# Last two output tiles before a layer norm by 256-token parts, feed-forward width in groups of 8, 6 and 8 chunks

## The chip, the cores and the metric

One core of a Trainium2 chip runs the whole program. The metric is the device time of one execution in microseconds. In the program and the rows PE is the tensor engine, PEld its weight load, DVE VectorE, ACT ScalarE, POOL GpSimd and SP the engine that issues most transfers.

## What is computed

Two blocks in a row on 512 tokens of width 1,024. The first has depth 2; each layer is feed-forward, mixer (state space, forgetting attention, short convolution), feed-forward, each followed by a layer norm of the residual sum:

```python
def layer_norm(x, g, b):
    xf = x.astype(jnp.float32)
    mu = jnp.mean(xf, axis=-1, keepdims=True)
    var = jnp.mean(jnp.square(xf - mu), axis=-1, keepdims=True)
    return ((xf - mu) * lax.rsqrt(var + LN_EPS) * g + b).astype(x.dtype)
...
def modulate(x, shift, scale):
    return x * (1.0 + scale) + shift
...
def swiglu_ffn(h, w_in, w_out):
    gate, up = jnp.split(h @ w_in, 2, axis=-1)
    return (jax.nn.silu(gate) * up) @ w_out
...
        h = modulate(x, mod[:, 0, 0], mod[:, 0, 1])
        y = swiglu_ffn(h, ffn1_w_in[l], ffn1_w_out[l])
        x = layer_norm(ALPHA * x + 0.5 * mod[:, 0, 2] * y, ln_g[l, 0], ln_b[l, 0])
```

The feed-forward is 2,816 wide, 22 chunks of 128. The second block has two layers, grouped-query attention and latent attention, each with a squared-relu feed-forward of width 4,096; its first layer also carries a context stream of 256 tokens. `mod` comes from a product of a vector with large modulation weights (`ada`).

## The kernel before

**Layout.** Activations lie transposed, 128 rows of the width by all tokens; a chunk is 128 rows, and there are 8. Each product is made of three passes over a split of both operands into a rounded part and its remainder (`passes`, L1934 to L1936), so weights and activations exist as `w_hi`, `w_lo`, `h_hi`, `h_lo`, `hid_hi`, `hid_lo`. A linear is a row of units of weights, each with `tpu` output tiles that are sums over `kc` chunks. For each unit a transfer brings `raw`, ScalarE rounds it (`w_hi`, L1262), VectorE subtracts (`w_lo`, L2750); there are two slots for weights, so unit i is rounded when unit i-2 has been used. The tiles leave PSUM by VectorE: L2817 or L3142 adds a tile times its gate to `x_lat`.

**Feed-forward.** The width is cut in groups (`FF_GROUPS`, 12 and 10 chunks). For each group a `gateup` linear makes the hidden chunks (ScalarE gate, VectorE product, ScalarE rounding, VectorE remainder `hid_lo` L2804), then an output linear of 8 tiles, one unit each, adds to `x_lat`. The last group's output linear ends in the norm. VectorE makes the partial sums of the modulation (`ada_acc`, L2833 and L2836) after each unit of the early linears; its last two units of a linear come in `finish`, behind the first units of the next linear. The tensor engine sums them (L1928) after the first and the second unit of the next linear.

**The norm.** Parts are 256 tokens: two of `lat`, and one of `ctx` where both streams run. Towards the end of the output linear GpSimd adds the first four tiles (`x_sum`), the tensor engine multiplies them by `ones` (`first_mean`, L1942), ScalarE copies that first mean, and VectorE subtracts it from x (`shifted`, L3015), so that squares can be made early: ScalarE squares, GpSimd adds squares (`ssum`). The last tile is computed by parts. `totals_begun` (L1950 to L1958) multiplies `x_sum`, `ssum` and the squares of tile 6 with `ones`; `close` (L1966, L1969) adds the last tile and its squares. VectorE then has mean and variance (`deviation`, L3053 to L3058), ScalarE the root, VectorE the reciprocal (L3065), then centred and scaled groups of chunks (L3076, L3087), ScalarE `h_hi`, GpSimd the same in full (L1056), VectorE `h_lo` (L3095). The next linear begins with part 0 on the first chunks of `h_lo` (`after_norm`); inside its chunk 3 the totals of part 1 are closed.

**The context step** (`ctx_in`, VectorE's `context_in`) prepares the context's first input between the two linears of the last feed-forward group of the first block. It waits for all modulation sums counted up to its place. Before a linear that feeds a norm, VectorE waits for `x` of all parts (`x_ready`); before another linear right behind the context step the wait leaves out the context's part (`parts_behind`).

Each engine runs its own program in written order; semaphores join them.

## Time and profile before

| | us |
|---|---|
| median of three runs | 3,999.8 |
| lowest and highest run | 3,988.89 and 3,999.96 |
| span of the profiled execution, first to last instruction | 3,992.6 |
| tensor engine busy in it | 3,831.8 |
| mean granted clock of the tensor engine | 0.978 |

The span is that of one execution; 7.2 us lie between it and the median of the runs. A busy tensor engine is one that has a multiplication in it. Idle time of an engine is printed in brackets before the instruction that ended it, with the instruction that released it.

### The profile page before, as it was taken

To read this page: it belongs to the slowest core of one execution; us is meant where nothing else is said; L and a number is where in the kernel's file an instruction comes from. 1 tells how busy PE (TensorE), PEld (TensorE's weight loads), DVE (VectorE), ACT (ScalarE), POOL (GpSimd) and SP (SyncE) were. 2 spreads that over 40 slices of the span, in tenths; PEclk is the share of its full clock that TensorE was granted. 3 is DMA by queue.
4 is the path that set the end of the run, shared out by engine and by line. 5 is a ranking of instruction groups with operands and counts; after the bars stand their busy time and mean duration, and the time that the engine had idled before them with its cause. 6 is when DMAs were issued, how large, how long until landed. Compare 5 with 4: busy or idle time off the path is not lost.

```text
span 3992.6 us, 51437 instructions
## 1 busy us (share of the span) xinstructions
PE 3831.8 (96%) x20234; PEld 3226.3 (81%) x20234; DVE 2539.0 (64%) x4095; ACT 1385.7 (35%) x1994; POOL 561.8 (14%) x559
## 2 busy tenths in 40 slices
PE   8999999999999999999998988989999999999998
PEld 6888877888888888788887678878888887888886
DVE  4666776754674677778445489686665367866335
ACT  2222334322232224432123179431221234853223
POOL 1000402300120012130004200150000141113001
PEclk8999999999999999999999999999999989999999
DMA  4554212344343432125322011213322112322221
GB/s 186 191 212 162 85 64 75 137 142 171 131 157 137 163 122 75 43 95 187 140 79 86 11 28 29 82 62 118 127 109 105 56 48 63 71 77 85 95 95 64
DMA packets 71229, 415.97 MB, mean 104 GB/s; under 512 B 8928, under 2 KB 12128, under 8 KB 30048
## 3 DMA queue, kind: packets, MB, share of 16 engines
q1 hardware_dynamic: 69744, 406.63, 29.3%
q10 hardware_dynamic: 1264, 6.29, 0.4%
q8 instruction: 151, 2.47, 0.3%
q14 instruction: 70, 0.57, 0.0%
HBM read 391.92 MB, written 2.10 MB: 99 GB/s over the span
## 4 chain that ended last, share of the span: by engine, by line
PE 81%; DVE 13%; ACT 2%; issue 2%; POOL 2%; DMA 0%; DVEq 0%; ACTq 0%; POOLq 0%
PE ps L1934 25%; PE ps L1936 24%; PE ps L1935 24%; DVE nmax L3716 2%; PE ps L1928 1%; DVE w_lo L2750 1%; PE ps L2644 1%; POOL sq_h_lat L1056 1%; DVE gp_lo L3733 1%; DVE rstd_lat L3065 1%; DVE x_lat L3076 1%; DVE x_lat L3087 1%; DVE mp_lo L3733 1%; DVE gprob L3728 1%; PE ps L2173 1%
## 5 line engine op out<-in xcount | busy, mean ns | idle before, releaser
L1934 PE MATMUL ps<-h_hi,w_lo 128*128 128x512 f32 (+2 forms) x2872 | 1096.6, 382 | 71.5 <-DVE h_lo L3095 49.6
L1936 PE MATMUL ps<-h_hi,w_hi 128*128 128x512 f32 (+2 forms) x2872 | 1073.0, 374 | 0.0
L1935 PE MATMUL ps<-h_lo,w_hi 128*128 128x512 f32 (+1 forms) x2800 | 1046.3, 374 | 0.0
L1262 ACT ACTIVATE w_hi<-raw 128x2048 fp32r<-128x2048 f32 (+3 forms) x262 | 457.8, 1748 | 1367.7 <-PE ps L1936 1329.7
L2750 DVE TENSOR_TENSOR w_lo<-raw,w_hi 128x2048 fp32r<-128x2048 f32 (+3 forms) x262 | 558.5, 2132 | 576.4 <-ACT w_hi L1262 576.1
L1934 PEld LDWEIGHTS ps<-h_hi,w_lo 128*128 128x128 f32 (+1 forms) x2872 | 548.9, 191 | 181.4 <-DVE h_lo L3095 46.0
L1936 PEld LDWEIGHTS ps<-h_hi,w_hi 128*128 128x128 f32 (+1 forms) x2872 | 548.3, 191 | 95.8
L1935 PEld LDWEIGHTS ps<-h_lo,w_hi 128*128 128x128 f32 x2800 | 535.5, 191 | 87.4 <-issue 0.5
L2836 DVE SCALAR_TENSOR_TENSOR ada_acc<-raw,c_act,ada_acc 128x256 f32<-128x256 f32 x1141 | 499.9, 482 | 16.8
L1934 PE MATMUL ps<-hid_hi,w_lo 128*128 128x512 f32 (+1 forms) x1272 | 498.9, 392 | 8.7 <-DVE w_lo L2750 6.8
L1936 PE MATMUL ps<-hid_hi,w_hi 128*128 128x512 f32 (+1 forms) x1272 | 490.2, 385 | 0.0
L1935 PE MATMUL ps<-hid_lo,w_hi 128*128 128x512 f32 (+1 forms) x1272 | 489.8, 385 | 0.0
L1934 PEld LDWEIGHTS ps<-hid_hi,w_lo 128*128 128x128 f32 x1272 | 240.1, 189 | 62.8 <-DVE w_lo L2750 8.9
L1936 PEld LDWEIGHTS ps<-hid_hi,w_hi 128*128 128x128 f32 x1272 | 239.7, 188 | 51.6
L1935 PEld LDWEIGHTS ps<-hid_lo,w_hi 128*128 128x128 f32 x1272 | 240.2, 189 | 50.4 <-issue 1.2
L1027 POOL TENSOR_TENSOR x_sum_lat<-x_lat 128x512 f32<-128x512 f32 x10 | 14.1, 1412 | 1867.2 <-DVE x_lat L3142 1319.4
L3142 DVE SCALAR_TENSOR_TENSOR x_lat<-ps,mod_lat,x_lat 128x512 f32<-128x512 f32 x70 | 52.4, 749 | 183.4 <-PE ps L1936 177.7
L1056 POOL TENSOR_SCALAR sq_h_lat<-x_lat,mod_lat 128x256 f32<-128x256 f32 x144 | 132.8, 931 | 173.5 <-DVE x_lat L3087 173.5
L3716 DVE TENSOR_REDUCE nmax<-ps 128x1 f32<-128x768 f32 x160 | 134.7, 842 | 8.2 <-PE ps L1936 5.7
L1304 ACT ACTIVATE hid_hi<-val_t 128x512 f32 (+1 forms) x88 | 55.6, 632 | 225.2 <-DVE val_t L2798 225.2
L1934 PE MATMUL ps<-hc_hi,w_lo 128*128 128x256 f32 x424 | 122.5, 289 | 8.2 <-DVE hc_lo L3095 8.2
L1440 ACT ACTIVATE h_hi<-x_lat,mod_lat 128x256 fp32r<-128x256 f32 x144 | 79.7, 594 | 128.8 <-DVE x_lat L3087 128.8
(486 smaller groups left out, 5969.8 us busy)
## 6 DMA issues: line engine op xcount, KB each, us to landing
raw<-ada SPq DMA_DIRECT2D x114, 1024.0 KB, 4.9
raw<-ffn_in SPq DMA_DIRECT2D x87, 1024.0 KB, 6.7
raw<-mlp_in SPq DMA_DIRECT2D x32, 1024.0 KB, 4.9
raw<-mlp_out SPq DMA_DIRECT2D x32, 1024.0 KB, 5.0
raw<-ffn_out SPq DMA_DIRECT2D x32, 768.0 KB, 5.4
raw<-ffn_out SPq DMA_DIRECT2D x32, 640.0 KB, 3.9
raw<-mix_p SPq DMA_DIRECT2D x14, 1024.0 KB, 4.8
raw<-mix_x SPq DMA_DIRECT2D x8, 1024.0 KB, 5.0
```

Of the source, the lines that this page charges most:

```text
L1056: eng.tensor_scalar(h32[:, k, part.cs], x[:, k, part.cs], g[:, k:k + 1], b[:, k:k + 1], ALU.mult, ALU.add).then_inc(s_n32, 1)
L1262: eng.activation(w_hi[:, slot, 0:ln.width], raw[:, slot, 0:ln.width], ACT.Copy).then_inc(s_whi, 1)
L1304: eng.activation(hid_hi[:, at(i), :], val_t[:, pos % 2, 0:SEQ].unsqueeze(1), ACT.Copy)\
L1440: eng.activation(hi[:, k, part.cs], x[:, k, part.cs], ACT.Identity, bias=b[:, k:k + 1], scale=g[:, k:k + 1]).then_inc(s_nhi, 1)
L1934: eng.matmul(out, lo_w, hi_x, start=first, stop=False, skip_group_check=True)
L1935: eng.matmul(out, hi_w, lo_x, start=False, stop=False, skip_group_check=True)
L1936: return eng.matmul(out, hi_w, hi_x, start=False, stop=last, skip_group_check=True)
L2750: eng.tensor_tensor(w_lo[:, slot, 0:ln.width], raw[:, slot, 0:ln.width], w_hi[:, slot, 0:ln.width].bitcast(F32), ALU.subtract).then_inc(s_ ...
L2836: ins = eng.scalar_tensor_tensor(acc, weights[:, :, k, :], c_act[:, c:c + 1], acc, ALU.mult, ALU.add)
L3142: a = eng.scalar_tensor_tensor(x, ps[:, tile_bank(ln, m, st), 0:NT[st]], MODT[st][:, ln.gate[st], 2 * DC + m:2 * DC + m + 1], x, ALU.mult, ...
L3716: eng.reduce_max(nmax[:, k % 8:k % 8 + 1], flat(2 * (k % 2))[:, 0:nk], AX_X, negate=True).then_inc(t_mx, 1)
L3733: eng.tensor_tensor(a.p[1][:, k % NPT, :], ps[:, B_PT + k % 2, :], a.p[0][:, k % NPT, :].bitcast(F32), ALU.subtract).then_inc(t_pl, 1)
```

## The change

- In every linear that feeds a norm, tiles 6 and 7 (before: only 7) are computed by parts: both tiles of part 0, then both of part 1, and of the context where there is one. Their evacuation, squares and closing sums become two per part (`last_tile`, `square_last`, `close_sum`, `close_squares`); tile 6 leaves `x_sum`, and `totals_begun` loses its third product. Part 0's totals are begun inside tile 6 of part 1. The tiles' sums are closed at chunk 3 of the next linear, the squares at chunk 4.
- `FF_GROUPS` is 8, 6, 8. Three pairs of linears in place of two; the last output linear has two tiles to a unit of 2,048 columns. No linear of the feed-forward is long enough for a loop any more.
- The first mean is taken in tile 4 ahead of its chunk 6 (before: behind tile 4); the shifts of pairs 0, 1 and 3 stand ahead of tile 4's evacuation.
- The modulation units keep their total; they fall on other linears. The context step comes behind the second group's `gateup`, whose six units all carry modulation units of two vectors, and ahead of an output linear that doesn't feed a norm.

```diff
 FF = 2816
-FF_GROUPS = (12, 10)
+FF_GROUPS = (8, 6, 8)
 FF2 = 4096
...
+def out_tiles(g):
+    return 2 if g + 1 == len(FF_GROUPS) else 1
 def schedule():
...
                 s.append(("ctx_in", Norm(None, None, 6, ("ctx",))))
-            lin(f"ffn{which}_out_{l}_{g}", DC, 1, nc, "resid", src="hid")
+            per = out_tiles(g)
+            lin(f"ffn{which}_out_{l}_{g}", DC // per, per, nc, "resid", src="hid")
...
-        def last_bank(ln, part):
-            if part.st == "ctx":
-                return 3
-            if len(ln.streams) == 1 and ln.norm.next and len(ln.norm.next.streams) > 1:
-                return 0 if part.c0 else 1
-            return 2 if part.c0 else tile_bank(ln, DC - 1, "lat") if len(ln.streams) > 1 else 3
+        def part_bank(ln, q, part):
+            nxt = ln.norm.next
+            if len(ln.streams) == 1 and nxt and len(nxt.streams) > 1:
+                return q if part.c0 else 2 + q
+            return tile_bank(ln, DC - 2 + q, part.st)
...
                            skip_group_check=True)
-                eng.wait_ge(s_sq, w.sq + 4 * ns)
+            def close_sum(norm, j):
+                part = norm.parts[j]
+                c = part.cs
+                eng.wait_ge(s_evac, part_evac(norm, j, 0))
+                eng.matmul(ps[:, B_SUM[j], 0:HALF], ones[:, :], X[part.st][:, DC - 2, c], start=False, stop=False,
+                           skip_group_check=True)
+                eng.wait_ge(s_evac, part_evac(norm, j, 1))
+                eng.matmul(ps[:, B_SUM[j], 0:HALF], ones[:, :], X[part.st][:, DC - 1, c], start=False, stop=True,
+                           skip_group_check=True).then_inc(s_total, 1)
+            def close_squares(norm, j):
+                part = norm.parts[j]
+                c = part.cs
+                eng.wait_ge(s_sq7, 2 * part.nidx + 1)
                 eng.matmul(ps[:, B_SQ, 0:HALF], ones[:, :], squares_of(norm, part.st)[:, DC - 2, c], start=False,
                            stop=False, skip_group_check=True)
-            def close(norm, j):
-                part = norm.parts[j]
-                c = part.cs
-                eng.wait_ge(s_evac, last_evac(norm, j))
-                eng.matmul(ps[:, B_SUM[j], 0:HALF], ones[:, :], X[part.st][:, DC - 1, c], start=False, stop=True,
-                           skip_group_check=True).then_inc(s_total, 1)
-                eng.wait_ge(s_sq7, part.nidx + 1)
+                eng.wait_ge(s_sq7, 2 * part.nidx + 2)
                 eng.matmul(ps[:, B_SQ, 0:HALF], ones[:, :], squares_of(norm, part.st)[:, DC - 1, c], start=False,
...
                             if p in norm.parts and k == 3 and closing:
-                                close(norm, closing.pop(0))
+                                close_sum(norm, closing[0])
+                            if p in norm.parts and k == 4 and closing:
+                                close_squares(norm, closing.pop(0))
                             if wide > 1 and n + 1 == len(parts):
...
                             eng.wait_ge(s_wlo2, ln.halved)
-                            eng.wait_ge(s_evac, last_evac(norm, 1))
+                            eng.wait_ge(s_evac, part_evac(norm, 1, 1))
                             for k in range(DC):
...
                                 slot = (ln.g0 + u) % 2
+                                if m == 4 and k == 6 and st == "lat":
+                                    first_mean(norm)
                                 mm = passes(ps[:, tile_bank(ln, m, st), 0:NT[st]], w_hi[:, slot, ws], w_lo[:, slot, ws],
...
                         mm.then_inc(s_tile, 1)
-                        if m == 4:
-                            first_mean(norm)
-                    u, q = divmod(DC - 1, ln.tpu)
-                    if q == 0:
-                        eng.wait_ge(s_wlo, ln.g0 + u + 1)
-                    eng.wait_ge(s_evac, ln.e0 + DC - ln.nbuf)
+                    eng.wait_ge(s_wlo, ln.g0 + ln.n)
                     for j, part in enumerate(norm.parts):
-                        if part.c0:
-                            eng.wait_ge(s_evac, tile_evac(norm, DC - 2))
-                        for k in range(ln.kc):
-                            if j == 1 and k == 2:
-                                close(norm, j - 1)
-                            mm = part_mm(u, q, part, k, last_bank(ln, part))
-                        mm.then_inc(s_tile if j + 1 == len(norm.parts) else s_last, 1)
-                        if j < 2:
-                            totals_begun(norm, j)
+                        for q in range(2):
+                            m = DC - 2 + q
+                            if j == 0:
+                                eng.wait_ge(s_evac, ln.e0 + m - ln.nbuf + 1)
+                            elif part_bank(ln, q, part) == part_bank(ln, q, norm.parts[j - 1]):
+                                eng.wait_ge(s_evac, part_evac(norm, j - 1, q))
+                            else:
+                                eng.wait_ge(s_evac, tile_evac(norm, DC - 3))
+                            for k in range(ln.kc):
+                                if j == 1 and q == 0 and k == 2:
+                                    totals_begun(norm, 0)
+                                    close_sum(norm, 0)
+                                if j == 1 and q == 0 and k == 4:
+                                    close_squares(norm, 0)
+                                mm = part_mm(ln.n - 1, q, part, k, part_bank(ln, q, part))
+                            mm.then_inc(s_tile if j + 1 == len(norm.parts) else s_last, 1)
+                        if j == 1:
+                            totals_begun(norm, 1)
                     if not norm.next:
-                        close(norm, len(norm.parts) - 1)
+                        close_sum(norm, 1)
+                        close_squares(norm, 1)
...
                     elif ln not in CUSTOM:
-                        linear(ln, sched[j - 1][1] if sched[j - 1][0] == "lin" else None, norm, before_it)
+                        prev = next(i for i in sched[j - 1::-1] if i[0] != "ctx_in")
+                        linear(ln, prev[1] if prev[0] == "lin" else None, norm, before_it)
                     if norm:
...
-            def shifted_sums(norm, k):
+            def shifted_sums(norm):
...
                 for i, st in enumerate(norm.streams):
-                    a = X[st][:, 4, :]
-                    if k == 5:
-                        eng.wait_ge(s_cent, w.cent + 2 * ns + 2 * i + 1)
-                    else:
-                        a = x_sum[st][:, :]
-                        eng.wait_ge(s_csum, w.csum + i + 1)
-                        eng.wait_ge(s_cent, w.cent + 4 * ns)
-                        eng.wait_ge(s_evac, tile_evac(norm, 6))
-                    eng.tensor_tensor(x_sum[st][:, :], a, X[st][:, k, :], ALU.add).then_inc(s_csum, 1)
-            def last_tile(ln, j):
-                part = ln.norm.parts[j]
-                x = X[part.st][:, DC - 1, part.cs]
-                if j == 0:
+                    eng.wait_ge(s_cent, w.cent + 3 * ns + i + 1)
+                    eng.tensor_tensor(x_sum[st][:, :], X[st][:, 4, :], X[st][:, 5, :], ALU.add).then_inc(s_csum, 1)
+            def last_tile(ln, j, q):
+                part, m = ln.norm.parts[j], DC - 2 + q
+                x = X[part.st][:, m, part.cs]
+                if j == 0 and q == 0:
                     eng.wait_ge(s_cent, w.cent + 4 * len(ln.norm.streams))
                 if j + 1 < len(ln.norm.parts):
-                    eng.wait_ge(s_last, w.last + j + 1)
+                    eng.wait_ge(s_last, w.last + 2 * j + q + 1)
                 else:
-                    eng.wait_ge(s_tile, ln.t0 + DC)
-                eng.scalar_tensor_tensor(x, ps[:, last_bank(ln, part), part.cs],
-                                         MODT[part.st][:, ln.gate[part.st], 3 * DC - 1:3 * DC], x, ALU.mult, ALU.add)\
+                    eng.wait_ge(s_tile, ln.t0 + m + 1)
+                eng.scalar_tensor_tensor(x, ps[:, part_bank(ln, q, part), part.cs],
+                                         MODT[part.st][:, ln.gate[part.st], 2 * DC + m:2 * DC + m + 1], x, ALU.mult, ALU.add)\
                    .then_inc(s_evac, 1)
...
                 parts = norm.parts
-                last_tile(ln, 0)
+                last_tile(ln, 0, 0)
                 if norm.next:
                     ahead(norm.next, 0, 1)
+                last_tile(ln, 0, 1)
                 deviation(norm, 0)
...
                             split_part(norm, part, g - 1)
-                        if g == 3 and j + 1 < len(parts):
-                            last_tile(ln, j + 1)
+                        if g == (1 if j == 0 and len(ln.streams) > 1 else 3) and j + 1 < len(parts):
+                            last_tile(ln, j + 1, 0)
+                            last_tile(ln, j + 1, 1)
                     if j + 1 < len(parts):
...
                         vectors_of(norm)
-                    elif m == 4:
-                        eng.wait_ge(s_evac, tile_evac(norm, 3))
-                        shifted(norm, (0, 1))
                     elif m == 5:
                         eng.wait_ge(s_evac, tile_evac(norm, 5))
-                        shifted(norm, (2, 3))
-                        shifted_sums(norm, 5)
-                    elif m == 6:
-                        shifted_sums(norm, 6)
+                        shifted(norm, (2,))
+                        shifted_sums(norm)
...
                     split_weights(ln, i, 0, i)
+                eng.wait_ge(s_evac, tile_evac(norm, 3))
+                shifted(norm, (0, 1, 3))
                 for m in range((ln.n - 2) * ln.tpu, (ln.n - 1) * ln.tpu):
                     tile(m)
-                for m in range((ln.n - 1) * ln.tpu, DC - 1):
-                    tile(m)
                 apply(ln, norm)
-                w.last += len(norm.parts) - 1
+                w.last += 2 * (len(norm.parts) - 1)
                 w.norm_done(norm)
```

The tensor engine at the first norm, from the end of part 0 of tile 7 (before), and there from inside part 1 of tile 6 (after; 6 products of it stand ahead of the first row). Names: `x_sum`, `ssum` are the sums made ahead, `x_lat,ones` a closing sum, `sq_h_lat,ones` one of squares. Before:

```order
L1950 MATMUL ps<-x_sum_lat,ones 128x256 [waits ln_shifted_summed]
L1955 MATMUL ps<-ssum_lat,ones 128x256 [waits ln_squares_summed]
L1958 MATMUL ps<-sq_h_lat,ones 128x256 [waits ln_squared]
L1934 MATMUL ps<-hid_hi,w_lo 128x256 [waits tile_evacuated]
L1935 MATMUL ps<-hid_lo,w_hi 128x256
L1936 MATMUL ps<-hid_hi,w_hi 128x256
L1934 MATMUL ps<-hid_hi,w_lo 128x256
L1935 MATMUL ps<-hid_lo,w_hi 128x256
L1936 MATMUL ps<-hid_hi,w_hi 128x256
L1966 MATMUL ps<-x_lat,ones 128x256 [waits tile_evacuated]
L1969 MATMUL ps<-sq_h_lat,ones 128x256 [waits ln_last_squared]
```

After:

```order
L1945 MATMUL ps<-x_sum_lat,ones 128x256 [waits ln_shifted_summed]
L1950 MATMUL ps<-ssum_lat,ones 128x256 [waits ln_squares_summed]
L1958 MATMUL ps<-x_lat,ones 128x256 [waits tile_evacuated]
L1961 MATMUL ps<-x_lat,ones 128x256 [waits tile_evacuated]
L1929 MATMUL ps<-hid_hi,w_lo 128x256
L1930 MATMUL ps<-hid_lo,w_hi 128x256
L1931 MATMUL ps<-hid_hi,w_hi 128x256
L1929 MATMUL ps<-hid_hi,w_lo 128x256
L1930 MATMUL ps<-hid_lo,w_hi 128x256
L1931 MATMUL ps<-hid_hi,w_hi 128x256
L1969 MATMUL ps<-sq_h_lat,ones 128x256 [waits ln_last_tiles_squared]
L1972 MATMUL ps<-sq_h_lat,ones 128x256 [waits ln_last_tiles_squared]
```

Line numbers of the same statement differ by a few. Behind part 0 came three opening products, six of part 1, and two closing ones; now two opening and two closing sums stand behind the first six, and two sums of squares behind the next six.

VectorE around the context step (`mod_ctx` to `hc_lo`). Before, from the last unit of the `gateup` linear:

```order
L2750 TENSOR_TENSOR w_lo<-raw,w_hi 128x1280 [waits weights_rounded]
L2798 TENSOR_TENSOR val_t<-ps,gate_t 128x512 [waits hidden_split,gate_activated]
L2804 TENSOR_TENSOR hid_lo<-val_t,hid_hi 128x512 [waits hidden_rounded]
L2992 TENSOR_TENSOR mod_ctx<-ps,par 128x24 [waits ada_unit_summed,ctx_loaded]
L2995 TENSOR_SCALAR mod_ctx<-mod_ctx 128x8 [waits modulation_steps]
L2997 TENSOR_SCALAR mod_ctx<-mod_ctx 128x8
L3095 TENSOR_TENSOR hc_lo<-sq_h_ctx,hc_hi 128x256 [waits h_modulated_of_part,h_rounded_of_part] x2
L3095 TENSOR_TENSOR hc_lo<-sq_h_ctx,hc_hi 128x512 [waits h_modulated_of_part,h_rounded_of_part] x3
L3142 SCALAR_TENSOR_TENSOR x_lat<-ps,mod_lat,x_lat 128x512 [waits tile_ready,x_ready_for_resid,tile_evacuated]
L2750 TENSOR_TENSOR w_lo<-raw,w_hi 128x1280 [waits weights_rounded]
```

After, from the second vector-pair modulation unit of `finish`:

```order
L2811 TENSOR_TENSOR val_t<-ps,gate_t 128x512 [waits hidden_split,gate_activated]
L2817 TENSOR_TENSOR hid_lo<-val_t,hid_hi 128x512 [waits hidden_rounded]
L2846 TENSOR_SCALAR ada_acc<-raw,c_act 128x256 [waits ada_unit_summed,weights_loaded_2]
L2846 TENSOR_SCALAR ada_acc<-raw,c_act 128x256
L2849 SCALAR_TENSOR_TENSOR ada_acc<-raw,c_act,ada_acc 128x256 [waits ada_partial_products] x14
L3005 TENSOR_TENSOR mod_ctx<-ps,par 128x24 [waits ada_unit_summed,ctx_loaded]
L3008 TENSOR_SCALAR mod_ctx<-mod_ctx 128x8 [waits modulation_steps]
L3010 TENSOR_SCALAR mod_ctx<-mod_ctx 128x8
L3101 TENSOR_TENSOR hc_lo<-sq_h_ctx,hc_hi 128x256 [waits h_modulated_of_part,h_rounded_of_part] x2
L3101 TENSOR_TENSOR hc_lo<-sq_h_ctx,hc_hi 128x512 [waits h_modulated_of_part,h_rounded_of_part] x3
L2763 TENSOR_TENSOR w_lo<-raw,w_hi 128x768 [waits weights_rounded,x_ready_for_resid,tile_evacuated]
L2830 SCALAR_TENSOR_TENSOR x_lat<-ps,mod_lat,x_lat 128x512 [waits tile_ready]
```

The step had nothing of the modulation ahead of it and a residual that waits for x behind it; now a modulation unit of two vectors stands right ahead, and behind it the split of a unit of 768 columns.

## Rows read from the trace of the kernel before

**Rows 1.** The page, part 1: busy us, share, instructions of each engine.

```profile
PE 3831.8 (96%) x20234; PEld 3226.3 (81%) x20234; DVE 2539.0 (64%) x4095; ACT 1385.7 (35%) x1994; POOL 561.8 (14%) x559
```

**Rows 2.** Waits of the tensor engine: total us, times, longest.

```profile
PE ps L1934 <- DVE h_lo L3095: 49.6, 42, 4.4
...
PE ps L1934 <- DVE w_lo L2750: 16.2, 7, 6.0
```

**Rows 3.** Timeline, tensor engine, first norm: start, us, operation, [idle before, releaser].

```profile
429.44 0.39 PE L1934 MATMUL ps<-hid_hi,w_lo 128*128 128x512 f32 x1
...
436.77 0.38 PE L1934 MATMUL ps<-hid_hi,w_lo 128*128 128x256 f32 x1 [0.20 <-DVE w_lo L2750]
...
440.42 0.59 PE L1950 MATMUL ps<-x_sum_lat,ones 128*128 128x256 f32 x2
...
440.85 0.59 PE L1955 MATMUL ps<-ssum_lat,ones 128*128 128x256 f32 x2
...
448.86 0.36 PE L1934 MATMUL ps<-h_hi,w_lo 128*128 128x256 f32 x1 [1.27 <-DVE h_lo L3095]
...
453.41 0.38 PE L1934 MATMUL ps<-h_hi,w_lo 128*128 128x256 f32 x1 [1.74 <-DVE h_lo L3095]
...
468.55 0.39 PE L1934 MATMUL ps<-h_hi,w_lo 128*128 128x256 f32 x1 [1.03 <-DVE h_lo L3095]
```

**Rows 4.** Timeline of VectorE in the same norm.

```profile
441.09 2.28 DVE L2750 TENSOR_TENSOR w_lo<-raw,w_hi 128x2048 fp32r<-128x2048 f32 x1
...
443.29 0.42 DVE L3053 TENSOR_SCALAR m_lat<-ps 128x256 f32<-128x256 f32 x1
...
444.20 0.42 DVE L3058 SCALAR_TENSOR_TENSOR rstd_lat<-ps,rstd_lat 128x256 f32<-128x256 f32 x1
...
456.66 0.42 DVE L3058 SCALAR_TENSOR_TENSOR rstd_lat<-ps,rstd_lat 128x256 f32<-128x256 f32 x1
```

**Rows 5.** Mixer norm: timeline; windows (PE, PEld, DVE, ACT, POOL busy; clock, DMA, GB/s).

```profile
705.67 0.60 PE L1950 MATMUL ps<-x_sum_lat,ones 128*128 128x256 f32 x2
...
722.40 0.42 DVE L3053 TENSOR_SCALAR m_lat<-ps 128x256 f32<-128x256 f32 x1 [1.32 <-PE ps L1966]
...
735.03 0.39 PE L1934 MATMUL ps<-h_hi,w_lo 128*128 128x256 f32 x1 [1.02 <-DVE h_lo L3095]
...
716.00:718.00 2.00, 1.59 (x6) 1.29 (x6) 1.36 (x3) 1.27 (x4) 2.00 (x3) 0.50 0.00 0
...
720.00:722.00 2.00, 2.00 (x10) 1.91 (x10) 1.07 (x2) 1.49 (x3) 1.43 (x2) 0.50 0.00 0
```

**Rows 6.** Timeline, end of a 12-chunk output linear: ScalarE, then VectorE.

```profile
917.91 1.92 ACT L1262 ACTIVATE w_hi<-raw 128x2048 fp32r<-128x2048 f32 x1 [6.88 <-PE ps L1936]
...
922.07 0.75 DVE L2817 SCALAR_TENSOR_TENSOR x_lat<-ps,mod_lat,x_lat 128x512 f32<-128x512 f32 x1
```

**Rows 7.** Timeline, start of a 10-chunk output linear: ScalarE, then VectorE.

```profile
1429.29 1.27 ACT L1262 ACTIVATE w_hi<-raw 128x1280 fp32r<-128x1280 f32 x1 [7.74 <-PE ps L1936]
...
1433.38 0.69 DVE L2804 TENSOR_TENSOR hid_lo<-val_t,hid_hi 128x512 fp32r<-128x512 f32 x1 [0.70 <-ACT hid_hi L1304]
...
1434.52 5.62 DVE L2836 SCALAR_TENSOR_TENSOR ada_acc<-raw,c_act,ada_acc 128x256 f32<-128x256 f32 x14
```

**Rows 8.** Timeline at the context step: three of VectorE, one of the tensor engine.

```profile
2091.70 0.18 DVE L2992 TENSOR_TENSOR mod_ctx<-ps,par 128x24 f32<-128x24 f32 x1
...
2098.05 0.93 DVE L3095 TENSOR_TENSOR hc_lo<-sq_h_ctx,hc_hi 128x512 fp32r<-128x512 f32 x1 [0.91 <-POOL sq_h_ctx L1056]
...
2104.70 0.75 DVE L3142 SCALAR_TENSOR_TENSOR x_lat<-ps,mod_lat,x_lat 128x512 f32<-128x512 f32 x1 [5.72 <-POOL x_ctx L1071]
...
2106.90 0.79 PE L1934 MATMUL ps<-hid_hi,w_lo 128*128 128x512 f32 x1 [5.96 <-DVE w_lo L2750]
```

**Rows 9.** Timeline, norm of both streams: tensor engine, then VectorE.

```profile
3203.11 0.59 PE L1950 MATMUL ps<-x_sum_lat,ones 128*128 128x256 f32 x2
...
3220.09 0.42 DVE L3058 SCALAR_TENSOR_TENSOR rstd_lat<-ps,rstd_lat 128x256 f32<-128x256 f32 x1
```

58 lines of the change are left out of this document (24 added, 34 removed).

## Prediction

> **What bounds the kernel now.** The page comes first: the tensor engine computes for 3,831.8 us of a 3,992.6 us span [rows 1], so only its idle time and the work put on it can move the time. The list of its waits says where the idle time lies: 49.6 us behind `h_lo` L3095, the last step of a layer norm, and 16.2 us behind `w_lo` L2750 [rows 2], of which one wait alone is 5.96 us, at the step that prepares the context [rows 8]. The feed-forward bodies between norms show no idle time worth a row. So the ten norms are what can be won, and the seams between linears, of which the change makes more, are what can be lost.
>
> A norm, read in the tensor engine's timeline [rows 3]: tile 6 of the output starts at 429.44; the first 256-token part of tile 7 runs from 436.77 to 440.42 (30 multiplications, 0.12 us each; a 512-token one starts every 0.23 us, 30 of them from 429.44); call its end T. Behind T come sums, the second part, sums again, and at 447.5 the engine is out of work. VectorE needs until 448.9 for the first `h_lo`, and the engine goes from wait to wait until 468.55. So from T+8.4 to T+28.1 the time is VectorE's chain, not the tensor engine's work. Two things move the end then: how early T comes, and how long the chain from T is.
>
> **The split of tiles 6 and 7.** T comes earlier, since half of tile 6 is put behind it. First norm: from the start of tile 6 to T there are 10.98 us [rows 3]. Groups of 8, 6, 8 make the last group 8 deep instead of 10, which moves 2 x 2 x 3 = 12 multiplications of 0.23 = 2.8 us elsewhere at no gain; afterwards two halves of 24 x 0.12 = 2.9, together 5.8. T is earlier by 10.98 - 2.8 - 5.8 = 2.4 us. With 8 chunks before and after: 8.4 before (24 x 0.23 + 24 x 0.12), so 2.6.
>
> The chain gets longer. (a) A multiplication with `ones` takes 0.43 us (one, in two instructions, from 440.42, the next from 440.85) [rows 3]. After T come now 6 products of tile 6 (0.7), `x_sum`, `ssum`, two closing sums (4 x 0.43 = 1.7), 6 products (0.7) and two sums of squares (0.9): 4.0 us, plus 0.3 to VectorE. Before, VectorE had the squares at 444.20, T+3.8 [rows 4]: +0.5. The 2.28 us `w_lo` that stood between last tile and mean [rows 4] now lies between the two last tiles and hides under the 2.9 us of products there, but the mean still waits for the sums, so nothing of it comes back. (b) VectorE adds a second last tile of part 1, 0.47: +0.5. (c) Part 1's sums are closed by the tensor engine inside the next linear, at its chunks 3 and 4. The third piece of `h_lo` lands at 453.4, T+13.0 [rows 3], now T+13.5; chunks 2 and 3 are 12 products (1.4), closing sum 0.9, then it waits for the fourth piece at T+16.4; chunk 4 is 0.7, the squares 0.9: T+18.0, with latency 18.2. VectorE would be there at 456.66 - 440.42 = 16.2 + 1.0 = T+17.2 [rows 4]. It waits 1.0. Sum: the chain is 2.0 us longer, last wait at T+30.1. The first norm gains 2.4 - 2.0 = 0.4 us.
>
> The mixer norm at 705.67 has 8 chunks before and after. It shows something else: at 716 and 720 the granted clock is 0.50, the lower level, 1.2 GHz, after the engine had sat idle in pieces from 712 on [rows 5]; its last wait ended at T+29.36 and VectorE waited 1.32 us for the engine's closing sum. With T 2.6 earlier and the last wait at T+30.1 at full clock, it gains 2.6 - 0.7 = 1.9. Four of the six norms that hand over to a 256-token part of one stream (the two mixers, the second feed-forward, the one after the second attention) show this drop; the two others don't. The stretch in which the engine mostly waits shrinks from six us (T+7 to T+13) to under four (T+9.9 to T+13.5), so I take the drop as gone except in one case in five. The Trainium skill (TensorE: Matmul & The Clock Gate, "HAM oscillation") prices a low stretch at half its length, here 3 us of at least 6; the rows say less, 29.36 against 28.13, 1.2 us, because the chain is VectorE's anyway. By the page the four norms would give 7 us more; the row decides.
>
> Sum for the ten norms: two first-type feed-forward norms 0.4 each; the second feed-forward norm, which had the drop, 1.8; mixers and latent attention 3 x 1.9; the one before the grouped attention 0 (a context part runs ahead of the closing, which puts VectorE 2.5 later and eats the 2.4); the last norm 1.3. That is 9.6. Less drops that stay or are new: -1.5.
>
> The two norms of **both streams** are different. T is earlier by 5.5 + 2.9 - 2.9 = 5.5 us, but the engine now has second part and context part behind it, 11.6 us with sums more, and comes to chunk 4 of the next linear, where part 1 is closed, at about T+22.5; before, VectorE had that at 3220.09 - 3203.11 = T+17.0 [rows 9]. 5.5 later: the gain is eaten by the place of the closing. Part 2 is closed the same way with two more products at 0.43 (0.86 at low clock) each for sum and squares: 1.5 to 2 later. I take -2 each, -4. Bounds: +3 (sums of squares ready in time and no drop) and -5.
>
> Norms together: 9.6 - 1.5 - 4 = **+4 us gained**.
>
> **The groups 8, 6, 8.** The products stay; 22 chunks are 22 chunks. What comes is one more seam in and out per feed-forward, four of each, and short linears.
>
> Out of a 6-chunk linear: its last tiles take 18 x 0.23 = 4.1. ScalarE rounds the next 2,048 columns from the end of tile 6 at 917.91 on, and VectorE has split them and evacuated tile 6 at 922.8, 4.9 later [rows 6]. An 8- or 12-chunk tile (5.5, 8.3) hides that; 4.1 doesn't. With 0.2 for the restart: 1.0 us, four times, **4.0**.
>
> Into a 6-chunk linear: the last hidden chunk was ready at 1434.07, 4.9 after the end at 1429.2 [rows 7]. With 768 columns rounding and splitting are 0.43 and 0.55 shorter: 3.9. The engine asks for chunk 6 after 15 x 0.23 = 3.4. 0.6 us each, in two plain seams **1.2**. In the third, whose modulation unit has two vectors, VectorE then spends 0.53 + 5.62 on it [rows 7] and is free at 10.1, while two tiles and a sum of 0.95 are through at 9.7; the engine waits 0.5 there and 0.7 more for tile 0's evacuation: **1.8**. The first feed-forward has a modulation unit with each tile of its 8-chunk linear, which gives VectorE nearly as much to do per tile as the tensor engine: **0.5** of lateness at the end, between 0 and 2.
>
> The fourth is the **context step**. Before: VectorE begins it at 2091.70, is through with `hc_lo` at 2098.98, then waits 5.72 for GpSimd's `x_ctx`, and the engine loses 5.96, with the restart 6.1 [rows 8]. Now the step stands before a linear that doesn't feed a norm, whose wait leaves the context part out, so the 5.72 is gone. But the six units ahead of it all carry modulation units of two vectors, and its first instruction waits for all of their sums; the last sum is made only after two tiles. Queue behind it on VectorE: the split of unit 2 and the evacuation of tile 0, for which the tensor engine waits. From the end of the last product: 0.6, VectorE free at 10.1, sum at 11.1, context step 7.3, split 0.95 and evacuation 0.7: 20.2. The engine was ready at 11.1: 9.1 lost, with 0.6 and 0.5 ahead of it 10.2. Net **4.1**.
>
> The **first mean** in the fifth tile, two chunks before its end, costs nothing: the sum of the first four tiles needs tile 3's evacuation and one addition of GpSimd, and the engine asks for it 18 x 0.23 = 4.1 us after tile 3. It keeps the shifts ahead of tile 4, where VectorE has slack. Loops that vanish cost or give nothing, since none shows in the rows.
>
> Costs: 4.0 + 1.2 + 1.8 + 0.5 + 4.1 = **11.6**. Net 7.6 slower: span 3,992.6 + 7.6 = 4,000.2. The median of three runs is 3,999.8, 7.2 over the span of the profiled execution; so 4,007.
>
> **Rivals.**
> Faster, *the chain isn't closed late*: if VectorE finds part 1's totals ready (engine at its chunk 4 earlier than I count), the eight one-stream norms give 2.6 - 1.0 each, 13, both-stream norms 3 each, 6, no clock drop 5: 24 - 11.6 = 12 faster, 3,988. For it: VectorE's chain was the bound everywhere. Against: at 722.40 it already waited 1.32 for that very sum [rows 5]. Chance 0.14.
> Slower, *closings at half clock*: one place, the closing of part 1 after T+13. If the engine falls to 1.2 GHz there, 12 + 6 products and four sums take double, VectorE gets the squares at T+21.4 instead of 18.2. 3.2 each; it decides from three norms on; in six of ten it is 17 to 19 in place of the 1.5: 4,023. For it: rows 5. Against: the shorter idle stretch. Chance 0.2.
> *The context step is cheap*: if its wait for the last sum fell under the two tiles, its 5.96 would go and nothing come: 10 better, 3,997, within the bound. Against: the order puts that sum behind tile 1. Chance 0.13.
> *The seams are free* (the 6-chunk tiles hide behind work I don't see): 5 better, 4,002. Chance 0.08.
> Forecast 0.45.
>
> **How the numbers follow.** About 0.3%, 12 us, is what a measurement here can tell from no change: 3,988 to 4,012. Faster than that: the first rival, 0.14. Slower: the second, 0.2, and the upper part of the forecast, 0.12, together 0.32. Same 0.54. The range takes in the bounds of both-stream norms (+10, -2), of the seams (-5) and three clock drops (+10): 3,989 to 4,023.
>
> **What would show it.** In the profile after: `h_lo` waits of the tensor engine fall in the one-stream norms (about 4 us each in place of 5), with the first wait (1.3) gone; VectorE waits for the closing squares of part 1; granted clock 1.00 through most norms; four waits on `w_lo` or `x_lat` of about 1 us where a 6-chunk linear ends; 9 us idle at the context step. It is wrong if the context step costs under 6 us, if the last wait of the first norm ends before T+29, or if the seams show no wait.

## The result and the profile after

| | before | after |
|---|---|---|
| median, us | 3,999.9 (4 runs) | 4,032.7 (4 runs) |
| lowest and highest run | 3,988.9 and 4,000.4 | 4,031.0 and 4,039.1 |
| profiled execution: span | 3,992.6 | 4,028.9 |
| tensor engine busy | 3,831.8 | 3,846.1 |
| mean granted clock | 0.978 | 0.979 |

The ratio is 1.0098 with an interval of 1.0086 to 1.011: 34 to 44 us slower. The forecast was 4,007 with a range up to 4,023, so the time lies outside it on the slow side. The spans differ by 36.3: 14.3 more busy and 22.0 more idle.

The page, part 1, of the changed kernel (to be read against [rows 1]):

```profile
PE 3846.1 (95%) x20494; PEld 3243.5 (81%) x20494; DVE 2532.9 (63%) x4141; ACT 1391.3 (35%) x2020; POOL 573.8 (14%) x559
```

Its waits of the tensor engine (total us, times, longest), against [rows 2]:

```profile
PE ps L1929 <- DVE h_lo L3101: 40.9, 38, 4.4
...
PE ps L1929 <- DVE x_lat L2830: 17.3, 9, 9.3
PE ps L1929 <- DVE w_lo L2763: 9.5, 2, 4.7
PE ps L1950 <- POOL ssum_lat L1047: 9.4, 7, 1.4
...
PE ps L1950 <- POOL ssum_ctx L1047: 6.1, 2, 3.1
...
PE ps L1929 <- DVE hid_lo L2817: 3.9, 4, 1.4
```

The waits for `h_lo` fell by 8.7 us and those for `w_lo` by 6.7. In their place stand 17.3 for evacuations (`x_lat`), 3.9 for hidden chunks, and 15.5 (9.4 and 6.1) for something that the list before did not have at all: GpSimd's sum of squares, `ssum`.

The first norm, tensor engine (start, us, operation, [idle before, releaser]); it answers to [rows 3]:

```profile
445.10 0.28 PE L1929 MATMUL ps<-hid_hi,w_lo 128*128 128x256 f32 x1
...
445.81 0.59 PE L1945 MATMUL ps<-x_sum_lat,ones 128*128 128x256 f32 x2
447.74 0.70 PE L1950 MATMUL ps<-ssum_lat,ones 128*128 128x256 f32 x2 [1.34 <-POOL ssum_lat L1047]
...
460.20 0.58 PE L1929 MATMUL ps<-h_hi,w_lo 128*128 128x256 f32 x1 [1.74 <-DVE h_lo L3101]
...
465.24 0.59 PE L1972 MATMUL ps<-sq_h_lat,ones 128*128 128x256 f32 x2
...
477.67 0.39 PE L1929 MATMUL ps<-h_hi,w_lo 128*128 128x256 f32 x1 [1.03 <-DVE h_lo L3101]
```

VectorE (first two rows) and GpSimd (last two rows) in the same norm, against [rows 4]:

```profile
439.60 0.75 DVE L3148 SCALAR_TENSOR_TENSOR x_lat<-ps,mod_lat,x_lat 128x512 f32<-128x512 f32 x1 [2.11 <-PE ps L1931]
...
450.99 0.42 DVE L3064 SCALAR_TENSOR_TENSOR rstd_lat<-ps,rstd_lat 128x256 f32<-128x256 f32 x1 [0.69 <-PE ps L1972]
...
438.12 2.67 POOL L1047 TENSOR_TENSOR ssum_lat<-ssum_lat,sq_h_lat 128x512 f32<-128x512 f32 x2
443.05 4.64 POOL L1047 TENSOR_TENSOR ssum_lat<-ssum_lat,sq_h_lat 128x512 f32<-128x512 f32 x2 [2.25 <-ACT sq_h_lat L1415]
```

The same in the kernel before, VectorE's evacuation of tile 5 and GpSimd's two additions:

```profile
429.64 0.75 DVE L3142 SCALAR_TENSOR_TENSOR x_lat<-ps,mod_lat,x_lat 128x512 f32<-128x512 f32 x1 [2.21 <-PE ps L1936]
...
433.64 4.23 POOL L1042 TENSOR_TENSOR ssum_lat<-ssum_lat,sq_h_lat 128x512 f32<-128x512 f32 x2 [2.25 <-ACT sq_h_lat L1410]
```

T, the end of part 0, is 445.10. Tile 5 starts to leave PSUM at 439.60. Its shift, squares and GpSimd's two additions (4.64) end at 447.69, 8.1 us later; the product that needs them is due 6.7 us after 439.60. Before, the additions ended 8.2 us after tile 5 as well (437.87), but the product came only 11.2 us after it (440.85), since a whole tile 6 lay between. The squares reach VectorE at T+5.9, the last wait ends at T+32.6.

Windows of 2 us, two in the same norm and one behind the context step (busy time of PE, PEld, DVE, ACT, POOL; clock; DMA share; GB/s):

```profile
461.00:463.00 2.00, 2.00 (x11) 2.00 (x11) 1.82 (x3) 1.02 (x3) 0.57 (x1) 0.50 0.00 0
463.00:465.00 2.00, 2.00 (x12) 1.83 (x12) 0.59 (x2) 2.00 (x3) 0.90 (x2) 0.86 0.02 4
...
2016.00:2018.00 2.00, 2.00 (x6) 1.59 (x5) 0.00 (x0) 0.00 (x0) 2.00 (x3) 0.50 0.63 194
```

The clock is at its lower level right behind the 1.74 us wait, where the closing sums of part 1 stand. In the profile of the kernel before this norm held full clock. That does not show that the change brought the drop: the profile of experiment 4, whose first norm is the old one, has the drop too (granted clock 0.50 from 460 to 462). The third window is read below.

Six waits at seams, tensor engine (the first two at the first output linear, which carries modulation units; out of a 6-chunk linear; into the last output linear; into the 6-chunk linear behind a modulation unit of two vectors; behind the context step):

```profile
196.31 0.47 PE L1929 MATMUL ps<-hid_hi,w_lo 128*128 128x512 f32 x1 [0.82 <-DVE x_lat L2830]
205.36 0.77 PE L1929 MATMUL ps<-h_hi,w_lo 128*128 128x512 f32 x1 [2.89 <-DVE x_lat L2830]
...
311.84 0.47 PE L1929 MATMUL ps<-h_hi,w_lo 128*128 128x512 f32 x1 [0.90 <-DVE x_lat L2830]
...
407.86 0.50 PE L1929 MATMUL ps<-hid_hi,w_lo 128*128 128x512 f32 x1 [0.98 <-DVE hid_lo L2817]
...
1337.14 0.47 PE L1929 MATMUL ps<-hid_hi,w_lo 128*128 128x512 f32 x1 [0.57 <-DVE x_lat L2830]
...
2014.52 0.77 PE L1929 MATMUL ps<-hid_hi,w_lo 128*128 128x512 f32 x1 [9.29 <-DVE x_lat L2830]
```

### The profile page after: what moved, and what is told of

Same layout as the page of the kernel before. It is cut to its first block, busy times and chain, and to the rows that moved or that the text cites. A ratio compares the mean times of both kernels' runs of the same rounds, so it can differ in the third digit from the quotient of the medians.

```text
span 4028.9 us, 50754 instructions
## 1 busy us (share of the span) xinstructions
PE 3846.1 (95%) x20494; PEld 3243.5 (81%) x20494; DVE 2532.9 (63%) x4141; ACT 1391.3 (35%) x2020; POOL 573.8 (14%) x559
## 3 DMA queue, kind: packets, MB, share of 16 engines
q8 instruction: 163, 2.67, 0.3%
## 4 chain that ended last, share of the span: by engine, by line
PE 79%; DVE 13%; POOL 3%; ACT 3%; issue 2%; DMA 1%; DVEq 0%; ACTq 0%; SPq 0%; POOLq 0%
PE ps L1929 24%; PE ps L1931 23%; PE ps L1930 23%; DVE nmax L3717 2%; PE ps L1923 1%; PE ps L2656 1%; POOL ssum_lat L1047 1%; DVE gp_lo L3734 1%; POOL sq_h_lat L1061 1%; ACT w_hi L1267 1%; DVE w_lo L2763 1%; DVE mp_lo L3734 1%; DVE rstd_lat L3071 1%; DVE gprob L3729 1%; DVE x_lat L3082 1%
## 5 line engine op out<-in xcount | busy, mean ns | idle before, releaser
L1930 PE MATMUL ps<-h_lo,w_hi 128*128 128x512 f32 (+2 forms) x2816 | 1049.2, 373 | 0.0
L1930 PEld LDWEIGHTS ps<-h_lo,w_hi 128*128 128x128 f32 (+1 forms) x2816 | 538.5, 191 | 88.2 <-issue 1.0
L1929 PE MATMUL ps<-hid_hi,w_lo 128*128 128x512 f32 (+1 forms) x1312 | 507.4, 387 | 16.7 <-DVE x_lat L2830 10.9
L1929 PEld LDWEIGHTS ps<-hid_hi,w_lo 128*128 128x128 f32 x1312 | 248.0, 189 | 69.8 <-DVE w_lo L2763 10.2
L2830 DVE SCALAR_TENSOR_TENSOR x_lat<-ps,mod_lat,x_lat 128x512 f32<-128x512 f32 x112 | 82.7, 745 | 88.2 <-PE ps L1931 88.0
L1309 ACT ACTIVATE hid_hi<-val_t 128x512 fp32r<-128x512 f32 x88 | 55.6, 632 | 212.9 <-DVE val_t L2811 212.9
```

What stands on the lines that cost most here:

```text
L1309: eng.activation(hid_hi[:, at(i), :], val_t[:, pos % 2, 0:SEQ].unsqueeze(1), ACT.Copy)\
L1929: eng.matmul(out, lo_w, hi_x, start=first, stop=False, skip_group_check=True)
L1930: eng.matmul(out, hi_w, lo_x, start=False, stop=False, skip_group_check=True)
L2830: a = eng.scalar_tensor_tensor(xm, tile, MODT[st][:, ln.gate[st], at(m + 2 * DC)], xm, ALU.mult, ALU.add)
```

## Experiments

Four or more runs each, in groups on one chip; the kernel before beside them had medians of 3,993.5 (1 to 4), 3,993.4 (5 to 8), 3,993.9 (9 to 11), 3,994.1 (12), 3,996.0 (13 and 14) and 3,992.7 (15 and 16). Runs of one kernel spread by 5 to 20 us, so a difference of a few us between two medians of four or five runs is uncertain by about as much; where it matters, the text says what the trace shows beside it.

**1. The groups alone.**

```diff
-FF_GROUPS = (12, 10)
+FF_GROUPS = (8, 6, 8)
-            lin(f"ffn{which}_out_{l}_{g}", DC, 1, nc, "resid", src="hid")
+            lin(f"ffn{which}_out_{l}_{g}", DC // per, per, nc, "resid", src="hid")
```

> The kernel before with the feed-forward groups 8, 6, 8 alone (last output linear two tiles to a unit, context step and modulation units where the change puts them); tiles 6 and 7, first mean and closings as before. Theory A: the 36 us of the changed kernel have two sources of like size; the groups cost about 20 (waits on x_lat at the ends of 6-chunk linears 8, on hid_lo into the last linears 4, lateness and low clock at the first feed-forward's first output linear 6.5, context step 3), the split of the tiles the other 13: 4,020. Theory B, as predicted: the groups cost 11.6 and the split is worth 4: 4,011, and the changed kernel's further 20 come from something in the split that was not priced. Theory C: the groups cost all of it, 4,033 or more.

4,016.5, ratio 1.0054 (1.0035 to 1.0074): 23 us over the kernel before on that chip. Both parts of the change cost, the groups more than half. Theory A stands; its cost of 20 was 3 short.

**2. The sum of squares multiplied later.** In `totals_begun` the product of `ssum` goes, in `close_squares` it comes first:

```diff
             def close_squares(norm, j):
+                eng.wait_ge(s_ss, w.ss + 5 * ns)
...
+                eng.matmul(ps[:, B_SQ, 0:HALF], ones[:, :], ssum[part.st][:, c], start=True, stop=False,
+                           skip_group_check=True)
```

> The changed kernel, but the product of the sum of squares (ssum) with ones stands behind the closing sums, right ahead of the squares of the two last tiles, in place of ahead of the closing sums. Theory A: the tensor engine waits there 9.4 us (one stream) and 6.1 us (both streams) for GpSimd's sum of squares, and this is the head of VectorE's chain; with the product later, 1.0 to 1.3 us come back in each of nine norms: 9 to 12 us faster than the changed kernel, 4,022. Rival: the chain needs the squares anyway and the wait only moves to the same place: within 3 us of the changed kernel, 4,030 or more.

4,021.5, ratio 1.0078 (1.0054 to 1.0102). The changed kernel had 1.0098 and, in the next group, 1.0097, so this is about 8 us faster by the ratios and 9 to 11 by the medians. The intervals overlap, as the four runs here range from 4,014.5 to 4,034.0. Tensor engine and VectorE in the first norm:

```profile
445.40 0.59 PE L1945 MATMUL ps<-x_sum_lat,ones 128*128 128x256 f32 x2
...
447.41 0.64 PE L1966 MATMUL ps<-ssum_lat,ones 128*128 128x256 f32 x2
...
449.03 0.42 DVE L3064 SCALAR_TENSOR_TENSOR rstd_lat<-ps,rstd_lat 128x256 f32<-128x256 f32 x1 [1.17 <-PE ps L1972]
```

The `ssum` product has no wait any more, and VectorE has the squares 3.6 us after the `x_sum` product in place of 5.2. In the norms of both streams 1.8 us of waiting for `ssum_ctx` are left of 6.1. Every stretch from one norm to the next (from the third evacuation of the linear that feeds the one to that of the linear that feeds the other) is 0.2 to 4.6 us shorter than in both profiles of the changed kernel. The late sum of squares is shown as a cause; its price is known to a few us only.

**3. First mean behind tile 4.**

```diff
-                                if m == 4 and k == 6 and st == "lat":
-                                    first_mean(norm)
...
+                        if m == 4:
+                            first_mean(norm)
```

> The changed kernel with the tensor engine's first mean behind tile 4 as before, in place of ahead of its chunk 6; the shifts stay ahead of tile 4's evacuation on VectorE. Theory A: 3.1 us of waits for GpSimd's x_sum go, but the mean comes 1.4 us (one stream) to 2.8 us (both) later to VectorE, which then has three shifts and two evacuations before the last shift: it takes 0 to 1.5 us a norm, 4,033 to 4,045. Rival (as predicted, the place costs nothing): 4,030 to 4,033.

4,037.1, ratio 1.011 (1.0092 to 1.0129), 6 us above the changed kernel in the next group, with intervals that overlap. The waits for `ssum_lat` grew from 9.4 to 11.9. Inside tile 4 is the better place once `ssum` is late.

**4. The kernel before without one wait.**

```diff
-                x_ready()
+                x_ready(int(ln.norm.name == "b1_1_2"))
```

> The kernel before, where VectorE's wait for x ahead of the linear behind the context step leaves out the context's part, which that linear does not touch. It shows what a context step costs whose only fault is that wait. Theory A: the 5.72 us wait goes and the tensor engine's 5.96 with its low clock: 5 to 7 us faster than the kernel before, 3,994. Rival: the split of unit 2 behind the step is late anyway: less than 2 us.

3,987.6 in ten runs, ratio 0.9983 (0.9972 to 0.9993): 6 us faster. The `w_lo` waits fell from 16.2 [rows 2] to 10.4, and at the step itself 0.15 us of idle time is left where 5.96 stood. Nearly all that the old context step cost was that wait.

**5. The changed kernel again.**

> The changed kernel itself once more, beside the three that follow, so that their differences are taken on one chip. Theory A and every rival: 4,031 to 4,036; first h_lo wait of the first norm, the ssum wait of 1.34 and the low clock behind it as in the first profile.

4,030.8, ratio 1.0097 (1.008 to 1.0114). Its rows in the first norm are the same to 0.1 us (waits of 1.33, 0.76, 1.73 and 0.48).

**6. Groups alone, last output linear in units of one tile.**

```diff
 def out_tiles(g):
-    return 2 if g + 1 == len(FF_GROUPS) else 1
+    return 1
```

> Groups alone (as in the first experiment, 4,016.5), but the last output linear of a feed-forward has one tile to a unit of 1,024 columns, as before, in place of two of 2,048. Theory A: the tensor engine's four waits on hid_lo at the start of that linear (0.98, 0.99, 0.54, 1.43 and 0.2 each for the restart, 4.6 together) come from the 2,048 columns that ScalarE rounds (1.92) and VectorE splits (2.29) ahead of the last hidden chunk, where 1,024 take 1.06 and 1.22; they shrink to 0.2 or less: 4,012 to 4,013. Rival: the waits come with the 8 chunks (24 products of 0.23 cover less than 30): less than 1 us of gain.

4,035.7, ratio 1.0103 (1.0086 to 1.012): 19 us slower than experiment 1, where a gain of 4 was expected. Both theories missed. The four waits on `hid_lo` are indeed gone from the trace, so they do come with the units of 2,048 columns. But in each of the four norms behind these linears there is a new one (VectorE, then GpSimd, then the tensor engine):

```profile
1100.67 2.36 DVE L3022 TENSOR_TENSOR x_lat<-x_lat,m_lat 128x1024 f32<-128x1024 f32 x2 [0.90 <-ACT m_lat L1407]
...
1106.24 3.84 DVE L3022 TENSOR_TENSOR x_lat<-x_lat,m_lat 128x1024 f32<-128x1024 f32 x2
...
1111.70 2.29 DVE L2757 TENSOR_TENSOR w_lo<-raw,w_hi 128x1024 fp32r<-128x1024 f32 x1
...
1105.46 7.44 POOL L1048 TENSOR_TENSOR ssum_lat<-ssum_lat,sq_h_lat 128x512 f32<-128x512 f32 x4
...
1114.05 0.58 PE L1940 MATMUL ps<-hid_hi,w_lo 128*128 128x256 f32 x1 [3.05 <-DVE w_lo L2757]
```

With one tile to a unit, the shifts, `x_sum` and the split of the last unit all fall between tile 5 and tile 7, in 11 us, beside GpSimd's additions; the same two shifts take 3.84 in place of 2.36. The kernel before has this order too, but with tiles of 6.9 us, and waits 0.20 there. The four new waits are 12 of the 19 us; where the rest lies was not traced. With 8 chunks the two-tile unit of the change is the better one.

**7. The first feed-forward back to 12 and 10**, three with 8, 6, 8.

```diff
+def groups_of(l, which):
+    return (12, 10) if (l, which) == (0, 1) else FF_GROUPS
```

> Groups alone, but the first feed-forward of the first layer keeps 12 and 10; the other three are 8, 6, 8. Theory A: the first feed-forward costs far more than the 2.1 us of the prediction, because VectorE has a split, an evacuation and a modulation unit to each tile of an 8-chunk linear: 9 us from its start to the norm's reciprocal in the traces, of which 5.2 on waits behind that linear, 2.4 on the other two seams, the rest in the norm: 4,007 to 4,009. Rival (the prediction's price): 4,014.

4,008.0 in ten runs, ratio 1.0029 (1.002 to 1.0039): 8.6 less than experiment 1 by the medians, 10 by the ratios. Theory A stands. One feed-forward of four carries more than a third of what the groups cost.

**8 and 9. Products that nobody reads, in the waits of the one-stream norms.** Ahead of a wait for `h_lo`:

```diff
+                    def fill(n):
+                        for _ in range(n):
+                            eng.matmul(ps[:, B_SUM[0], 0:HALF], w_hi[:, slot, 0:P], w_lo[:, slot, 0:HALF],
+                                       start=True, stop=True, skip_group_check=True)
...
+                                    fill(((0, 6, 14, 0, 0), (0, 3, 7, 2, 0))[n][GROUP_OF[k]])
```

> The changed kernel with the sum of squares' product later (the second experiment, 4,021.5), and in the five one-stream norms that hand over to a 256-token part 32 more products of 256 columns, whose sums nobody reads, on the tensor engine ahead of its waits for h_lo: 6 and 14 in part 0, 3, 7 and 2 in part 1. They add no wait for anything. Theory A: the clock falls because the engine sits idle in pieces; with the gaps filled it stays at 1.00, and as the chain is VectorE's, it is worth 0.5 to 1.5 us a norm: 4 to 8 us faster, 4,014 to 4,018. Rival 1: the clock doesn't fall less, and 0.1 to 0.5 us of overshoot a norm come on top: 4,022 to 4,025. Rival 2: the clock stays up but nothing is gained: within 2 us.

> As the filler experiment before it (4,015.0), but the 32 extra products of each one-stream norm go to the bank of part 0's sums, which VectorE has read by then, instead of to a bank in which the next linear's own sums are being formed. Theory A: the same products at the same places, the same time within the spread: 4,012 to 4,018, no low clock in the five norms. Rival: the bank matters, and the gain seen there came with it: 4,020 or more.

4,015.0 and 4,015.4, ratios 1.0055 (1.0038 to 1.0073) and 1.0051 (1.0033 to 1.0069), against 1.0078 without them: 6.5 us by the medians, with intervals that overlap. The products stand in six norms (192 of them in the trace); the expectation says five. In 8 they went to a PSUM bank in which the next linear's sums were being formed, and disturbed them; 9, whose diff stands above, uses a free bank. The two times agree, so the bank is no part of the gain. Windows of experiment 2, then of experiment 9, in the first norm (which comes 8.4 us later in the second profile), each with the first wait for `h_lo` behind them:

```profile
460.00:462.00 2.00, 2.00 (x7) 1.63 (x7) 1.22 (x3) 1.60 (x3) 1.48 (x2) 0.50 0.01 4
462.00:464.00 2.00, 2.00 (x10) 1.83 (x9) 0.60 (x2) 1.39 (x2) 0.00 (x0) 0.69 0.00 0
...
465.63 0.39 PE L1929 MATMUL ps<-h_hi,w_lo 128*128 128x256 f32 x1 [0.48 <-DVE h_lo L3101]
```

```profile
468.00:470.00 2.00, 1.78 (x12) 1.33 (x11) 1.91 (x4) 1.21 (x3) 1.15 (x2) 1.00 0.00 0
470.00:472.00 2.00, 2.00 (x15) 1.84 (x14) 0.41 (x2) 1.78 (x2) 0.56 (x1) 1.00 0.02 4
...
472.88 0.38 PE L1929 MATMUL ps<-h_hi,w_lo 128*128 128x256 f32 x1 [0.49 <-DVE h_lo L3109]
```

The same chain, at 0.50 without and 1.00 with the products. Counted from the `x_sum` product behind part 0 (445.40 and 453.78) the wait comes after 20.2 us without and 19.1 with them: the clock drop costs this norm 1.1 us. That fits the 6.5 in six norms. In the profile of experiment 2 the clock falls to 0.50 in all six, in those of 8 and 9 in none, and behind five of the six norms the stretch to the next is 0.6 to 1.4 us shorter (0.4 to 0.5 longer behind the first). But two stretches whose norms have none of these products are 4 us longer each than in experiment 2's profile, and why was not found; so for this kernel the gain of the whole is likely and not certain.

**10. The same in the kernel before**, with experiment 4's edit (6 and 12 products in part 0; 2, 7 and 2 in part 1).

> The kernel before without the wait for the context's part (as in the fourth experiment, 3,987.6) and with the extra products in its five one-stream norms: 6 and 12 in part 0, 2, 7 and 2 in part 1. Theory A (the clock drops of those norms cost 0.5 to 1.5 us each, whatever the tiles): 3,981 to 3,986. Rival: only the changed kernel's norms gain, since in the kernel before VectorE's chain has slack behind the tensor engine's: 3,987 or more.

3,979.9 in ten runs, ratio 0.9967 (0.9953 to 0.9981), 7.6 us below experiment 4, which had ten runs too: the fastest kernel here. Experiment 4's profile has the drop in all six norms, this one in none, and the stretch from one norm to the next is 1.0 to 1.4 us shorter behind five of the six (0.4 longer behind the first). Its norms behind the two mixers, which fell to 0.50 before [rows 5], hold 1.00, as here behind the first one:

```profile
722.00:724.00 2.00, 1.84 (x16) 1.64 (x14) 1.39 (x2) 1.26 (x3) 2.00 (x3) 1.00 0.04 8
```

**11. Groups alone, context step one pair later**, with experiment 4's edit.

```diff
-            if (l, which, g) == (1, 2, 1):
+            if (l, which, g) == (1, 2, 2):
```

> Groups alone (4,016.5), with the context step one pair of linears later, between the two linears of the last group as in the kernel before, and VectorE's wait for the context's part left out there; the modulation sums are long made by then. Theory A: the step's own work (7.3 us of VectorE) is hidden but for under 1 us, so that the 9.3 us wait, 0.4 of restart and a stretch at low clock (3) go: 4,004 to 4,006. Rival: VectorE is late with the step wherever it stands, and the fourth experiment's remainder comes back here: 4,010 or more.

4,002.8 in ten runs, ratio 1.0026 (1.0014 to 1.0039): 13.7 less than experiment 1, 1.2 more gain than the expectation's upper end. Its waits on `x_lat`:

```profile
PE ps L1940 <- DVE x_lat L2824: 9.8, 10, 3.0
```

against 19.0, with one of 9.3, in experiment 1.

**12. Both repairs**: first feed-forward 12 and 10, context step late.

> Groups alone, with both repairs: the first feed-forward keeps 12 and 10, and the context step stands between the last two linears without the wait for the context's part. Against the kernel before with that wait left out (3,987.6) it differs only by 8, 6, 8 in three feed-forwards. Theory A (the three causes add up): the seams of one feed-forward cost 1.1 (out of the 6-chunk linear), 0.15 (into it) and 1.15 (into the last), 2.4 each, 7 in all, and 4,016.5 - 8.6 - 13.7: 3,994 to 3,995. Rival: the repairs overlap, or the norms behind 8 chunks cost something of their own (shorter tiles, clock): 3,998 or more.

3,994.1 in ten runs, ratio 1.0005 (0.999 to 1.0019). The expectation was 3,994 to 3,995. The three causes of the groups' cost add up, as far as medians that are known to 2 or 3 us can tell.

**13. Squares closed in chunk 3** (experiment 2, and):

```diff
                                 close_sum(norm, closing[0])
-                            if p in norm.parts and k == 4 and closing:
                                 close_squares(norm, closing.pop(0))
```

> The changed kernel with the sum of squares' product later (the second experiment, 4,021.5), and part 1's (and part 2's) squares closed inside chunk 3 of the next linear, right behind the sums, as before, in place of chunk 4. The prediction blamed this place. Theory A: VectorE has the squares 0.7 us earlier in each norm and its second reciprocal with them, most of which reaches the tensor engine in nine norms: 3 to 6 us faster, 4,016 to 4,018. Rival: the tensor engine then stands at chunk 3 for ScalarE's squares (two, 0.4 each, behind VectorE's two evacuations) and gains nothing: 4,020 to 4,023.

4,017.5, ratio 1.0055 (1.0042 to 1.0069), 4.0 us under experiment 2 by the medians and 9 by the ratios, but the intervals overlap; the direction is theory A's. In the first norm the last wait ends 28.5 us after the `x_sum` product behind part 0 in place of 30.9, and the clock holds 1.00.

**14. The extra product alone**, on experiment 1: tile 6 left out of `x_sum`.

```diff
+                eng.matmul(ps[:, B_SUM[j], 0:HALF], ones[:, :], X[part.st][:, DC - 2, c], start=False, stop=False,
+                           skip_group_check=True)
...
-                        shifted_sums(norm, 6)
```

> Groups alone (4,016.5) with one piece of the split by itself: tile 6 is left out of x_sum (VectorE's addition of 0.7 to 0.9 goes) and multiplied by ones on the tensor engine, one product of 256 columns more for each of 22 parts, 0.43 each, 9.5 together. The tiles stay whole up to tile 6. Theory A: the products of part 0 and part 1 stand on the chain or ahead of the next linear's work, so that half or more of the 9.5 shows: 4,020 to 4,026, and the split's cost beyond the late sum of squares is these products. Rival: they fall into the tensor engine's waits and VectorE's relief pays for them: 4,015 to 4,018.

4,015.8, ratio 1.0053 (1.0039 to 1.0067), the same as experiment 1. Theory A falls: 22 products of 0.43 do not show. That VectorE's addition, which goes in return, pays for them is the rival's reason and was not separated.

**15 and 16. Groups alone, and 13, side by side.**

> Groups alone again (4,016.5 in four runs), to be compared with the next on one chip and in more runs. Theory A: 4,015 to 4,019.

> The changed kernel with both repairs of the closings again (4,017.5 in five runs). In the profiles, counted from the first gate of the first feed-forward, it is 10 us ahead of groups alone; in the medians 1 behind, and the start up to that gate differs by 8 us between profiled executions of any kernel. Theory A: the split, repaired, gains 1 us in each one-stream norm and loses nothing in those of both streams, 4,007 to 4,011. Rival: it gains nothing, what comes at the start of the chain is given back at its second half and in the clock: within 3 us of the run beside it.

4,018.4, ratio 1.0062 (1.0048 to 1.0076), and 4,014.3, ratio 1.0052 (1.0038 to 1.0066). Over both times of each, 9 runs have a mean of 4,017.5 and 10 runs one of 4,015.2. By all runs the split with both faults repaired gains about 2 us in ten norms, within the spread of either; theory A's 4,007 to 4,011 is not reached. The profiles say more: counted from the first gate of the first feed-forward to the end, the repaired split takes 3,921.9 and 3,922.0 (experiments 13 and 16), the groups alone 3,932.0 and 3,930.1 (1 and 15). With one profile a run it stays open how much of these 8 to 10 us is scatter.

## Why the prediction was wrong, point by point

**The groups: 11.6 predicted, 23 measured (experiment 1).** The sign was right and so were most kinds of cost; one seam was missed and several sizes were off.

- *Out of a 6-chunk linear, 1.0 each.* Right: 0.90 idle (row at 311.84), and 1.30 from start to start in place of 0.23, so 1.07, four times.
- *Into a 6-chunk linear, 0.6, and 1.8 behind the unit of two vectors.* Too much: two of the tensor engine's products stood 0.38 apart there in place of 0.23, and the second kind of seam has that and a wait of 0.57 (row at 1337.14).
- *Missed: into the last output linear.* It starts with a unit of 2,048 columns and not 1,280 as before, and ScalarE and VectorE handle those before the last hidden chunk: 0.98 idle (row at 407.86), 3.9 in the four. The prediction priced only seams into linears of 6 chunks. Experiment 6 shows the columns as the cause.
- *The first feed-forward: 0.5 for lateness.* This term failed; with its two seams the prediction had 2.1 there, experiment 7 gives 8.6. VectorE needs 1.23 for the split, 0.75 for the evacuation and 3.95 for the modulation unit, 5.9 us to a tile, and the tensor engine 5.5 and a sum of 0.35: as long. The prediction said "nearly as much" and then took the middle of "between 0 and 2". What VectorE falls behind at each of eight tiles adds up: it came as waits of 0.17, 0.82 and 2.89 (rows at 196.31 and 205.36), then a stretch at half clock (granted clock 0.50 from 206 to 210).
- *The context step, net 4.1.* The mechanism was right: the step waits for the last modulation sum, with a split and an evacuation queued behind it, and the tensor engine idles 9.29 where 9.1 were predicted. Its size is less sure. The old step was priced at 6.1 and is worth 6 (experiment 4). The new one was priced at 10.2, and taking it away gave 13.7 by the medians (experiment 11), net 7.7; but the stretch between the norms around it, measured as in experiment 2, got only 10.2 shorter in that profile (405.2 in the mean of experiments 1 and 15, 395.0 in 11). The new wait is followed by products at half clock (window 2016 to 2018), which the sum left out; the old one was too (0.50 from 2106 to 2110), so this can explain a part of the difference only.

With 6.6 for the seams of the other three feed-forwards (experiment 12 against 4), 8.6 and 7.7 make 22.9 by the medians.

**The norms: a gain of 4 predicted, a loss of 14 by the medians measured (experiments 1 and 5; 17 by the ratios).**

- *T comes 2.4 earlier, the chain gets 2.0 longer.* The first half holds: part 0 of tiles 6 and 7 takes 5.7 us (439.40 to 445.10), where 5.8 were predicted. The chain got 4.4 longer, from T+28.1 to T+32.6. The prediction counted the tensor engine's products and VectorE's steps behind T. It never asked when GpSimd's `ssum` is ready, although `totals_begun` waits for it: its row does not stand among the ones read, since before it was done in time. Half of tile 6 put behind T took that cover away: the change moved T earlier and left another input of the same sums where it was. Price: 8 to 11 us (experiment 2), one-stream waits of 1.34, up to 3.1 with both streams.
- *The chunk-4 closing makes VectorE wait.* It did: squares predicted at T+18.0, closed at T+20.6 (the row at 465.24 and one product of 0.43). Of these 2.6 us 1.6 is the late start; the rest fits the half clock. Experiment 13 gives 4 us for undoing it, not certain.
- *The clock drop is gone except in one case in five.* Wrong. Of the four norms that showed a drop, three kept one of half the length and one lost it; the two others, the first (windows above) and the fourth, now show one. For these two the comparison is weak, since experiment 4's profile, with the old norms, has the drop in all six: which norm drops is partly a matter of the execution. The prediction read one execution. The chance given to "closings at half clock", 0.2, was too small, and it was treated as an alternative to the forecast rather than part of it.
- *First mean costs nothing.* It waits for GpSimd's `x_sum` three times, 2.4 us, but its old place would cost about 6 more (experiment 3): the place was worth something.
- *One-stream `h_lo` waits of about 4, first wait gone*: right (0.77, 1.74, 0.48 and 1.03 in the first norm). It says little about the time, as the waits had only moved.
- *Both-stream norms -2 each.* More, in the first of them: a wait of 3.0 us for `ssum_ctx`, then half clock. For the stretch from it to the next norm the changed kernel takes 598.6 and 598.4, the groups alone 593.5 and 591.3, and experiment 2 takes 594.0: 5 to 7 us, a third or more of the whole 14, in this one norm. The range counted at most 3 us of extra loss for it.

The split itself, both faults repaired, is worth about 2 us in ten norms by all runs (experiments 15 and 16) and 8 to 10 by the profiles; the runs do not settle which is nearer.

**The base.** The prediction put 7.2 us between span and median of three runs. Later medians of 9 to 20 runs of the kernel before lie at 3,992.7 to 3,996.0. The first gate of the first feed-forward comes at 87.4 in its profile, and between 83.7 and 92.9 in the others, whatever the kernel: start-up scatters by 9 us. Against the later medians the change costs 37 us and not 33; this is small beside the 26 by which the forecast missed.

**The range and the signs.** The line on the range gives the both-stream norms +10 and -2, where the bounds stated for each (+3 and -5 around -2) make 10 us faster and 6 slower. None of the three signs of being wrong came: the context step cost 9.3 idle, the last wait ended after T+29 and the seams showed waits. All three watch for a result faster than the forecast; no sign watched the slow side.

## What to carry to other kernels

When a step is moved earlier, list every semaphore that it waits for and ask of each whether its producer moves with it; the one that had slack before does not show in the list of waits. An engine that has as much work to a tile as the one that waits for it falls behind a little with each tile, and the sum is paid at the next seam. A short idle piece in front of work on the critical path can be filled with products that nobody reads, if a PSUM bank is free: here six norms gave 6 to 8 us by the medians, and 1.1 us in the one norm read above.

## What of the hardware was not expected

- The tensor engine's granted clock stayed at 1.00 through all six norms with 29 to 32 more products of 256 columns in each (experiments 8 to 10), where it fell to 0.50 in all six without them (2 and 4). No median rose with them.
- VectorE slowed beside GpSimd: two shifts of 1,024 columns 3.84 us in place of 2.36 and a split of 1,024 columns 2.29 in place of 1.23, while GpSimd's four additions took 7.44, 1.86 each, where two with little of VectorE beside them take 2.67, 1.33 each (row at 438.12). The Trainium skill (SBUF — State Buffer, "SBUF: two separate sides") says that a GpSimd operation and a VectorE operation with two inputs in SBUF share a pair of ports as an exclusive lock for a whole instruction; the trace agrees that both get slower, and does not show which waits.
- An extra product that starts a sum in other columns of a bank spoiled the sums under way in that bank: the result of experiment 8 is off by 0.85 of its size, and that of 9, in a free bank, is right. The Trainium skill (Advanced Engine Details and Errata, "PSUM Accumulation (`has_written` bits)") says that the first product of a sum clears, in the whole bank, the bits that tell later products to add rather than overwrite; that would do it.
